# Modulation vectors of a hybrid block: column sums on VectorE in place of chunk products on TensorE, low parts of the input stage on GpSimd

## The chip, the cores and the metric

One core of a Trainium2 chip runs the whole program. The metric is device time in microseconds, taken over runs of the kernel; a profiled execution gives the trace that the rows below come from.

## The reference, cut to what matters

Two layers, each a token mixer (state-space scan, pooling, attention) and a router with experts (PEER). What the change touches is the modulation: six vectors per layer of 1024 features, each a product of one conditioning vector with a matrix.

```python
cond = jax.nn.silu(c)                       # (1, 1024)
for l in range(DEPTH):                      # 2 layers
    mod = cond @ ada_w[l] + ada_b[l]        # 1024 x 6144
    sh1, sc1, g1, sh2, sc2, g2 = jnp.split(mod, 6, axis=-1)
    h = modulate(rms_norm(x, mix_norm_g[l]), sh1, sc1)      # h * (1 + sc) + sh
    mix = token_mixer(h, w_in[l], ...)                      # begins with h @ w_in
    x = x + g1[:, None, :] * mix
    h = modulate(rms_norm(x, ffn_norm_g[l]), sh2, sc2)
    x = x + g2[:, None, :] * peer_ffn(h, peer_wq[l], ...)
return rms_norm(x, final_norm_g)
```

There are 512 tokens of 1024 features. Features lie on the 128 partitions, in KT = 8 tiles.

## The kernel before

**Weights.** All products with weights are streamed in tiles of 128x1024 (`wst`, the loop of `load_w` on SyncE, three buffers `w_raw`). Each tile is split in two: ScalarE rounds it to a high part (`hi`, `w_hi`), and another engine subtracts to get the low part (`lo`, `w_lo`); both have two buffers, so the parts of tile n wait until TensorE has done tile n-2. A projection (`project`) is 24 products: high by high, high by low, low by high. The input stage is 18 such tiles per layer: 6 for the convolved channels, 2 for pooling, 4 for the gate z, 6 for attention. Tiles 0 and 1 are done together (`project_pair`), because they follow the normalised input `hH`, `hL` feature tile by feature tile. VectorE makes all low parts, except those of 37 tiles per layer in the gate stage that follows the router; there GpSimd makes them.

**What VectorE does in the input stage.** After tile n it runs step n: convolution (`conv`, n < 6), time steps (n = 4, 5: `time_step_exp`, `time_step_log`), scaled x (n = 6, 7: `x_scaled`), decay segments and scan matrices (`segments`, `scan_matrix`, n from 8 on), pooled means (n = 9 to 11) and attention scores. In each step it also makes the low part of tile n+2. TensorE takes the results between two tiles: `decay_sums` and `x_tokens` after tile 6, `scan_step` after tiles 9, 11, 13, 15, `pool_mixed` after tile 12.

**Modulation.** The six vectors are three sets of two. One set is 8 chunks of 128x2048 (1 MB). A chunk is multiplied on TensorE with one column of silu(c) repeated over 32 columns (`ada_chunk`), four matmuls into four column groups of a bank, summed over the chunks. ScalarE then copies the bank (`ada_rows`) and TensorE transposes it (`modulation`), since the sums lie along the free axis and are wanted along the partitions. Set 0 of layer 0 (shift and scale of the first normalisation) is needed before anything else: its chunks are loaded first, half of them from SyncE's queue and half from GpSimd's, and multiplied around the sums of squares. Sets 1 and 2 of layer 0 are 16 chunks, one after the first pair and one after nearly every projection of layer 0's input stage. All 24 chunks of layer 1 are done in layer 0: five in the gap before the router (the normalisation of the second half), nineteen between router tiles. Layer 1 has no chunks, and finds its vectors in `mod_raw`.

**Order.** Every engine's program is written out by hand and runs in order; semaphores join them. `unread` are matmuls whose results nobody reads, which fill TensorE's waits. On TensorE `s_tile` counts tiles done, on the others `s_wh` and `s_wl` the high and low parts.

## Time and profile before

| | us |
|---|---|
| median of three runs | 2833.79 |
| lowest of the runs | 2832.2 |
| the profiled execution | 2832.66 |
| its span on the core | 2830.8 |
| first products of the first pair begin | 38.75 |
| input stage of layer 0, from the end of the pair | 139.9 |
| the same of layer 1 | 123.9 |

The span runs from the first to the last instruction of the core; the profiled execution's own time has 1.9 us around it. Stages are read from the timeline of TensorE, whose order is fixed by the program: the first record of a kind in a stage gives its start.

### The profile page before, as it was taken

To read this page: it belongs to the slowest core of one execution; us is meant where nothing else is said; L and a number is where in the kernel's file an instruction comes from. 1 tells how busy PE (TensorE), PEld (TensorE's weight loads), DVE (VectorE), ACT (ScalarE), POOL (GpSimd) and SP (SyncE) were. 2 spreads that over 40 slices of the span, in tenths; PEclk is the share of its full clock that TensorE was granted. 3 is DMA by queue.
4 is the path that set the end of the run, shared out by engine and by line. 5 is a ranking of instruction groups with operands and counts; after the bars stand their busy time and mean duration, and the time that the engine had idled before them with its cause. 6 is when DMAs were issued, how large, how long until landed. Compare 5 with 4: busy or idle time off the path is not lost.

```text
span 2830.8 us, 49106 instructions
## 1 busy us (share of the span) xinstructions
PE 2788.0 (98%) x17864; PEld 2594.5 (92%) x17864; DVE 2494.8 (88%) x5020; ACT 1388.2 (49%) x2321; POOL 952.1 (34%) x773
## 2 busy tenths in 40 slices
PE   7999999999999999999999999999999999999998
PEld 4777789999999999999988788999999999999998
DVE  4667789999999799999987679999999979999998
ACT  3345225477777433333353532445777753333333
POOL 1000018833335244444400000694333434444342
PEclk9999999999999999999999999999999999999999
DMA  7434648999999899999932122699999999999996
GB/s 276 181 119 179 246 157 305 353 334 403 395 380 350 333 383 385 391 391 393 392 122 74 60 74 83 219 349 332 386 386 391 364 337 368 388 390 380 385 385 260
DMA packets 257144, 855.06 MB, mean 302 GB/s; under 512 B 26080, under 2 KB 59104, under 8 KB 250336
## 3 DMA queue, kind: packets, MB, share of 16 engines
q1 hardware_dynamic: 149280, 442.23, 42.3%
q0 software_dynamic: 98496, 381.73, 35.6%
q10 hardware_dynamic: 9216, 29.36, 2.6%
q8 instruction: 61, 1.00, 0.1%
q14 instruction: 91, 0.75, 0.1%
HBM read 777.06 MB, written 76.15 MB: 301 GB/s over the span
## 4 chain that ended last, share of the span: by engine, by line
PE 74%; DVE 12%; DMA 5%; issue 4%; POOL 2%; ACT 2%; SPq 0%; DVEq 0%; ACTq 0%; POOLq 0%
PE banks L1099 36%; PE banks L1633 9%; PE banks L1636 9%; PE banks L1640 9%; DMA w_raw<-wst 4%; PE banks L1597 3%; PE banks L1434 2%; DVE stages L2193 2%; DVE w_lo L1693 2%; DVE vacc L2205 1%; POOL w_lo L756 1%; PE banks L1171 1%; PE banks L1117 1%; POOL stages L769 1%; PE banks L1521 1%
## 5 line engine op out<-in xcount | busy, mean ns | idle before, releaser
L811 ACT ACTIVATE w_hi<-w_raw 128x1024 fp32r<-128x1024 f32 x596 | 628.4, 1055 | 635.7 <-PE banks L1099 322.8
L1693 DVE TENSOR_TENSOR w_lo<-w_raw,w_hi 128x1024 fp32r<-128x1024 f32 x522 | 638.0, 1222 | 236.4 <-ACT w_hi L811 189.8
L769 POOL DMA_INDIRECT ring<-v,gidx x320 | 393.5, 1230 | 612.9 <-DVE vacc L2205 523.5
L1099 PE MATMUL banks<-hH,w_hi 128*128 128x352 f32 (+1 forms) x2528 | 513.9, 345 | 0.6 <-ACT act_out L1025 0.5
L1099 PE MATMUL banks<-hH,w_lo 128*128 128x352 f32 (+1 forms) x2528 | 492.1, 336 | 2.2 <-DVE w_lo L1693 1.5
L1099 PE MATMUL banks<-hL,w_hi 128*128 128x352 f32 (+1 forms) x2528 | 491.4, 336 | 0.0
L1099 PEld LDWEIGHTS banks<-hH,w_hi 128*128 128x128 f32 x2528 | 416.2, 188 | 37.8 <-issue 10.8
L1099 PEld LDWEIGHTS banks<-hH,w_lo 128*128 128x128 f32 x2528 | 427.7, 188 | 22.9 <-DVE w_lo L1693 2.1
L1099 PEld LDWEIGHTS banks<-hL,w_hi 128*128 128x128 f32 x2528 | 428.1, 188 | 19.0
L769 POOL DMA_INDIRECT ring<-u,gidx x244 | 282.4, 1157 | 453.4 <-DVE gact L2193 442.5
L2205 DVE SCALAR_TENSOR_TENSOR vacc<-ring,gcoef,vacc 128x1024 f32<-128x1024 f32 x316 | 404.4, 1280 | 7.1
L756 POOL TENSOR_TENSOR w_lo<-w_raw,w_hi 128x1024 fp32r<-128x1024 f32 x74 | 178.2, 2408 | 407.5 <-PE banks L1099 406.5
L1636 PE MATMUL banks<-c_lo_late,w_hi 128*128 128x352 f32 x1520 | 273.3, 322 | 0.0
L1636 PEld LDWEIGHTS banks<-c_lo_late,w_hi 128*128 128x128 f32 x1520 | 247.6, 188 | 0.0
L1017 ACT ACTIVATE oneh<-oneh,gate_pow 128x128 bf16<-128x128 f16 x704 | 221.4, 392 | 4.2 <-ACT stages L1053 3.2
L1073 ACT ACTIVATE c_hi_late<-coef 128x352 fp32r<-128x352 f32 x128 | 63.9, 499 | 316.6 <-DVE coef L2402 316.6
L2193 DVE CUSTOM_DVE_ANT_0 ring<-ring,banks 128x1024 f32<-128x1024 f32 x180 | 214.4, 1212 | 0.1
L1633 PE MATMUL banks<-c_hi_first,w_hi 128*128 128x352 f32 x1024 | 183.8, 322 | 0.0
L1640 PE MATMUL banks<-c_hi_first,w_lo 128*128 128x352 f32 x1024 | 183.8, 322 | 0.0
L1633 PE MATMUL banks<-c_hi_late,w_hi 128*128 128x352 f32 x1008 | 181.4, 322 | 1.0 <-ACT w_hi L811 1.0
L1640 PE MATMUL banks<-c_hi_late,w_lo 128*128 128x352 f32 x1008 | 180.9, 322 | 0.0
L1073 ACT ACTIVATE c_hi_first<-coef 128x352 fp32r<-128x352 f32 x124 | 61.9, 499 | 240.6 <-DVE coef L2402 240.6
(360 smaller groups left out, 3923.0 us busy)
## 6 DMA issues: line engine op xcount, KB each, us to landing
w_raw<-wst SPq DMA_DIRECT2D x596, 512.0 KB, 6.6
activations<-act_out SPq DMA_DIRECT2D x124, 352.0 KB, 8.4
act_in<-activations SPq DMA_DIRECT2D x62, 704.0 KB, 7.3
gate_matrices<-stages ACTq DMA_DIRECT2D x64, 448.0 KB, 7.6
gates<-gate_matrices SPq DMA_DIRECT2D x64, 448.0 KB, 9.4
ada_buf<-adaw POOLq DMA_DIRECT2D x24, 1024.0 KB, 6.8
nrm<-adaw POOLq DMA_DIRECT2D x8, 1024.0 KB, 5.2
pj<-adaw POOLq DMA_DIRECT2D x7, 1024.0 KB, 7.1
```

The source lines that it names most:

```text
L756: pool.tensor_tensor(w_lo[g % 2][:, :, :].rearrange("p a b -> p (a b)"), w_raw[:, g % RAWS, :], w_hi[g % 2][:, :, :].rearrange("p a b -> p ...
L769: pool.indirect_dma_start(out=gather_slot(l, k), out_offset=None, in_=rows[:, :], in_offset=bass.IndirectOffsetOnAxis(ap=gidx[:, k % UG:k ...
L811: nc.scalar.activation(w_hi[g % 2][:, :, :].rearrange("p a b -> p (a b)"), w_raw[:, g % RAWS, :], ACT.Copy).then_inc(s_wh, 1)
L1017: ins = nc.scalar.activation(oh.bitcast(BF16), oh, ACT.Copy, scale=gate_pow[:, at:at + 1])
L1073: nc.scalar.activation(c_hi[(b + 2) % GROUP], coef[:, b % 2, :], ACT.Copy).then_inc(s_chi, 1)
L1099: last = mm(bank[s][:, 0:t.stop - t.start], a[s][:, k, :], b[:, k, t], start=(k == 0 and a is w_hi and b is hH), stop=(k == KT - 1 and a i ...
L1633: mm(bank[k][:, TG:T], w_hi[j % 2][:, k, :], c_hi[j], start=first, stop=False)
L1636: last = mm(bank[k][:, TG:T], w_hi[j % 2][:, k, :], c_lo[j], start=False, stop=False)
L1640: last = mm(bank[k][:, TG:T], w_lo[j % 2][:, k, :], c_hi[j], start=False, stop=False)
L1693: v.tensor_tensor(w_lo[g % 2][:, :, :].rearrange("p a b -> p (a b)"), w_raw[:, g % RAWS, :], w_hi[g % 2][:, :, :].rearrange("p a b -> p (a ...
L2193: v.tensor_tensor_reduce(row, row, rhs, 1.0, 0.0, ALU.mult, ALU.add, gact[:, k:k + 1]).then_inc(s_gd, 1)
L2205: ins = v.scalar_tensor_tensor(acc[:, :], row, gcoef[:, k:k + 1], acc[:, :], ALU.mult, ALU.add)
```

## The change

Three things are altered.

Set 0 of layer 0 comes in another order of its matrix: chunk k now holds, for all 1024 rows, the 128 shifts and 128 scales of feature tile k. `first_block(k)` multiplies it (32 matmuls of 64 columns), VectorE takes its values out of the bank by a masked sum (`first_scaled`) and scales feature tile k, and `first_pair` follows tile by tile. All eight chunks are loaded from SyncE's queue, after the first two weight tiles' place in it.

Sets 1 and 2 of both layers are no longer chunks on TensorE. Their matrix is stored transposed, feature on the partition, and silu(c) is spread over all partitions (`crow`). A `column_sum` on VectorE multiplies a row of 128x1024 with `crow` and sums it along the free axis, straight into a column of `mod_raw`. There are 32 per layer, in steps 2 to 15 of that layer's own input stage (`ROWS_AT`), and each row is loaded by SyncE between weight tiles (`ROW_LOAD`) into parts of `nrm`, `h32` and `pj`. Of layer 1's set 0 the eight chunks stay on TensorE in layer 0: five in the gap, three in the router.

The low parts of tiles 2 to 18 of each layer move from VectorE to GpSimd.

```diff
-ADA_CHUNKS = ADA_SETS * KT
+ADA_CHUNKS = KT
 ADA_BANK = ((7, 7, 7), (5, 6, 7))
-FIRST_ADA = (0, 2, 1, 4, 3, 6, 5, 7)
-assert sorted(FIRST_ADA) == list(range(KT))
+ADA_BLOCK = ADA_COLS // KT
+ADA_FOUR = ADA_BLOCK // 4
+FIRST_BANK = (7, 6, 4)
...
+LATER = 2 * ADA_COLS // P
+ROWS_AT = {2: 2, 3: 2, 4: 1, 5: 1, 6: 3, 7: 3, 8: 2, 9: 3, 10: 2, 11: 4, 12: 2, 13: 3, 14: 2, 15: 2}
...
+ROW_LOAD = {3: (0, 1), 4: (2, 3), 5: (4, 5), 6: (6, 7, 8), 7: (9, 10), 8: (11, 12), 9: (13, 14, 15), 10: (16, 17),
...
+        def row_home(j):
+            i = ROW_PLACE[j]
+            if i < 2:
+                return nrm[:, 2 * i:2 * i + 2, :].rearrange("p a t -> p (a t)")
+            if i < 4:
+                return h32[:, 2 * i - 4:2 * i - 2, :].rearrange("p a t -> p (a t)")
+            if i < 6:
+                return pj[:, Q0:Q0 + 4, :].rearrange("p a t -> p (a t)")[:, (i - 4) * D:(i - 3) * D]
+            return h32[:, 6:8, :].rearrange("p a t -> p (a t)") if i == 6 else h32[:, 4:6, :].rearrange("p a t -> p (a t)")
...
+            def load_rows(l, n):
+                if n == 3:
+                    if l > 0:
+                        sp.wait_ge(s_x, l * KT)
+                    else:
+                        sp.wait_ge(s_adat, KT)
+                    sp.wait_ge(s_rows, 2 * l + 1)
+                    sp.dma_start(crow[:, :], cB).then_inc(s_cin, 16)
+                if n == 5:
+                    sp.wait_ge(s_dtg, l + 1)
+                for j in ROW_LOAD[n]:
+                    if j >= 8:
+                        sp.wait_ge(s_mdot, l * LATER + row_before(j) + 1)
+                    sp.dma_start(row_home(j), adaw[l, KT + j // 2][:, j % 2 * D:(j % 2 + 1) * D]).then_inc(row_in(l, j)[0], 16)
...
-            for k in (1, 3, 5, 7):
+            for k in range(KT):
                 sp.dma_start(ada_place(k), adaw[0, k]).then_inc(s_ada0[k], 16)
-            load_w(0, 0)
-            load_w(0, 1)
+                if k == 0:
+                    load_w(0, 0)
+                    load_w(0, 1)
...
+                    if n in ROW_LOAD:
+                        load_rows(l, n)
...
-            for k in (0, 2, 4, 6):
-                pool.dma_start(ada_place(k), adaw[0, k]).then_inc(s_ada0[k], 16)
...
+                for n in range(2, OUT0 + 1):
+                    if n == 2:
+                        pool.wait_ge(s_wl, l * STREAM + 2)
+                    lo(l, n)
...
+                    if n == Q0:
+                        act.wait_ge(s_mdot, l * LATER + 12)
...
+                    if n == 1:
+                        act.wait_ge(s_cin, (l + 2) * 16)
+                        nc.scalar.activation(crow[:, :], crow[:, :], ACT.Silu).then_inc(s_cond, 1)
...
+                def first_block(k):
+                    pe.wait_ge(s_ada0[k], 16)
+                    for c in range(KT):
+                        for g in range(4):
+                            o = c * ADA_BLOCK + g * ADA_FOUR
+                            last = mm(bank[FIRST_BANK[k % 3]][32 * g:32 * g + 32, k * ADA_FOUR:(k + 1) * ADA_FOUR],
+                                      tiny[:, 0, c:c + 1].broadcast_to([P, 32]),
+                                      ada_place(k)[:, o:o + ADA_FOUR], start=(c == 0), stop=(c == KT - 1))
+                    last.then_inc(s_adat, 1)
+                def first_pair(k):
+                    if k == 0:
+                        pe.wait_ge(s_wh, 2)
+                        pe.wait_ge(s_wl, 2)
+                        pe.wait_ge(s_taken, 2)
+                    pe.wait_ge(s_rhs, k + 1)
+                    for s in range(2):
+                        for a, b in ((w_hi, hH), (w_hi, hL), (w_lo, hH)):
+                            last = mm(bank[s][:, :], a[s][:, k, :], b[:, k, :],
+                                      start=(k == 0 and a is w_hi and b is hH),
+                                      stop=(k == KT - 1 and a is w_lo))
+                        if k == KT - 1:
+                            last.then_inc(s_tile, 1)
...
                 if l == 0:
-                    for c in FIRST_ADA[0:3]:
-                        ada_chunk(0, c)
                     pe.wait_ge(s_const, 11)
-                norm_groups(2 * l)
-                if l == 0:
-                    ada_chunk(0, FIRST_ADA[3])
-                if l == 0:
-                    for c in FIRST_ADA[4:7]:
-                        ada_chunk(0, c)
-                if l > 0:
+                    unread(10)
+                    norm_groups(0)
+                    unread(4)
+                    first_block(0)
+                    norm_rows(0)
+                    unread(6)
+                    first_block(1)
+                    for k in range(KT):
+                        if k + 2 < KT:
+                            first_block(k + 2)
+                        first_pair(k)
+                else:
+                    norm_groups(2 * l)
                     unread(8)
-                norm_rows(2 * l)
-                if l == 0:
-                    unread(5)
-                    ada_chunk(0, FIRST_ADA[7])
-                    unread(3)
-                    modulation(0, 0, 4)
-                    unread(13)
-                else:
+                    norm_rows(2 * l)
                     unread(10)
-
-                project_pair(l, 0, l * RHS_PARTS)
-                if l == 0:
-                    ada_chunk(0, KT)
+                    project_pair(l, 0, l * RHS_PARTS)
...
-                    if l == 0 and n != KT + 1:
-                        ada_chunk(0, KT + n - 1 if n <= KT else KT + n - 2)
...
-                    pe.wait_ge(s_arow, ADA_SETS)
-                    modulation(0, 1, 7)
-                    modulation(0, 2, 7)
...
-                        for c in chunks_of(n):
-                            ada_chunk(1, c)
+                        if GAP_ADA + n < KT:
+                            ada_chunk(GAP_ADA + n)
                         if n == 7:
-                            modulation(1, 0, 4)
+                            modulation()
...
-                    modulation(1, 1, 4)
-                    modulation(1, 2, 4)
...
+            def first_modulated():
+                ada_b, g_mix = pcol("ada_b"), pcol("g_mix")
+                def first_scaled(k):
+                    dve.wait_ge(s_adat, k + 1)
+                    for m in range(2):
+                        o = k * ADA_FOUR + m * EXTRA
+                        ins = v.tensor_tensor_reduce(tiny[:, 9 + m, :], bank[FIRST_BANK[k % 3]][:, o:o + EXTRA], token_of[:, :], 1.0, 0.0,
+                                                     ALU.mult, ALU.add, tiny[:, 8, 2 * k + m:2 * k + m + 1])
+                    link(ins)
+                    v.tensor_scalar(mod[:, 0, k:k + 1], tiny[:, 8, 2 * k:2 * k + 1], ada_b[:, k:k + 1], None, ALU.add)
+                    link(v.scalar_tensor_tensor(gs[:, 0, k:k + 1], tiny[:, 8, 2 * k + 1:2 * k + 2],
+                                                ada_b[:, KT + k:KT + k + 1], g_mix[:, k:k + 1], ALU.add, ALU.mult))
+                    v.scalar_tensor_tensor(h32[:, k, :], x[:, k, :], gs[:, 0, k:k + 1], bank[2][:, :],
+                                           ALU.mult, ALU.mult).then_inc(s_nrm, 1)
+                dve.wait_ge(s_const, 16)
+                dve.wait_ge(s_rows, 1)
+                first_scaled(0)
+                lo(0, 1)
+                for k in range(KT):
+                    if k + 1 < KT:
+                        first_scaled(k + 1)
+                    dve.wait_ge(s_hh, k + 1)
+                    v.scalar_tensor_tensor(hL[:, k, :], h32[:, k, :], mod[:, 0, k:k + 1],
+                                           hH[:, k, :].bitcast(F32), ALU.add, ALU.subtract).then_inc(s_rhs, 1)
...
+                def column_sum(j):
+                    if j == 0:
+                        dve.wait_ge(s_cond, l + 2)
+                    dve.wait_ge(*row_in(l, j))
+                    row = row_home(j)
+                    v.tensor_tensor_reduce(row, row, crow[:, :], 1.0, 0.0, ALU.mult, ALU.add,
+                                           mod_raw[:, 2 * KT + j:2 * KT + j + 1]).then_inc(s_mdot, 1)
...
-                        lo(l, n + 2)
...
+                    for _ in range(ROWS_AT.get(n, 0)):
+                        column_sum(summed)
+                        summed += 1
...
+                dve.wait_ge(s_mdot, (l + 1) * LATER)
```

VectorE in layer 0's input stage, steps 2 to 4, before (L1693 is the low part; L1786 to L1791 a convolution; L1799 to L1803 the time steps):

```order
L1693 TENSOR_TENSOR w_lo<-w_raw,w_hi 128x1024
L1786 TENSOR_SCALAR xbc<-pj,par 128x512
L1789 SCALAR_TENSOR_TENSOR xbc<-pj,par,xbc 128x512 x2
L1791 SCALAR_TENSOR_TENSOR xbc<-pj,par,xbc 128x512
L1693 TENSOR_TENSOR w_lo<-w_raw,w_hi 128x1024
L1786 TENSOR_SCALAR xbc<-pj,par 128x512
L1789 SCALAR_TENSOR_TENSOR xbc<-pj,par,xbc 128x512 x2
L1791 SCALAR_TENSOR_TENSOR xbc<-pj,par,xbc 128x512
L1799 TENSOR_TENSOR tiny<-banks,par 128x32
```

The same place after (L1984 is a column sum and the read of its accumulator):

```order
L1835 TENSOR_SCALAR xbc<-pj,par 128x512
L1838 SCALAR_TENSOR_TENSOR xbc<-pj,par,xbc 128x512 x2
L1840 SCALAR_TENSOR_TENSOR xbc<-pj,par,xbc 128x512
L1984 ISA nrm,mod_raw<-nrm,crow 128x1024
L1984 ISA mod_raw 128x1
L1984 ISA nrm,mod_raw<-nrm,crow 128x1024
L1984 ISA mod_raw 128x1
L1835 TENSOR_SCALAR xbc<-pj,par 128x512
L1838 SCALAR_TENSOR_TENSOR xbc<-pj,par,xbc 128x512 x2
L1840 SCALAR_TENSOR_TENSOR xbc<-pj,par,xbc 128x512
L1984 ISA pj,mod_raw<-pj,crow 128x1024
L1984 ISA mod_raw 128x1
```

The low part of each step is gone from VectorE, and one to four column sums stand behind each step's own work.

GpSimd's queue after the constants, before: chunk loads up to the gate stage.

```order
L732 AFFINE_SELECT tri_lt<-tri_lt 128x128
L746 DMA nrm<-adaw 128x2048
L746 DMA pj<-adaw 128x2048
L746 DMA nrm<-adaw 128x2048
L746 DMA pj<-adaw 128x2048
```

And after: the input stage's low parts, then the loads of layer 1's eight chunks, then the gate stage's low parts.

```order
L764 AFFINE_SELECT tri_lt<-tri_lt 128x128
L778 TENSOR_TENSOR w_lo<-w_raw,w_hi 128x1024 x17
L771 DMA ada_buf<-adaw 128x2048 x3
L771 DMA pj<-adaw 128x2048 x2
L771 DMA ada_buf<-adaw 128x2048 x3
L778 TENSOR_TENSOR w_lo<-w_raw,w_hi 128x1024 x9
```

Seventeen low parts stand where loads stood, and 16 of the 24 loads for layer 1 are gone.

## Rows read from the trace of the kernel before

**Rows 1.** The page: busy time, share of span, instructions, by engine
```profile
PE 2788.0 (98%) x17864; PEld 2594.5 (92%) x17864; DVE 2494.8 (88%) x5020; ACT 1388.2 (49%) x2321; POOL 952.1 (34%) x773
```

**Rows 2.** Windows, input stages: length, PE, PEld, DVE, ACT, POOL busy; clock, DMA
```profile
51.40:191.30 139.90, 139.90 (x765) 99.87 (x764) 84.47 (x142) 54.30 (x69) 7.39 (x14) 1.00 0.47 174
1461.40:1585.30 123.90, 122.16 (x638) 98.29 (x638) 84.22 (x143) 52.02 (x67) 0.00 (x0) 1.00 0.21 73
```

**Rows 3.** Chain, then timeline (start, length): last chunk, first pair; square sums
```profile
4.51 26.39 DMA pj<-adaw
...
38.75 12.80 PE banks L1117 x48
...
21.44 2.72 PE L1131 MATMUL banks<-h,ones 128*32 128x128 f32 x64
```

**Rows 4.** Window at the start, ending in GB/s; landing of keys, of w_raw
```profile
8.00:10.00 2.00, 0.00 (x0) 0.00 (x0) 0.66 (x6) 0.72 (x2) 0.00 (x0) 1.00 1.02 434
...
DMA to landing us min/median/max: 4.8/4.8/4.8
...
DMA to landing us min/median/max: 3.1/6.6/27.9
```

**Rows 5.** Timeline of TensorE, layer 0: the first output block begins
```profile
207.55 0.47 PE L1434 MATMUL banks<-hH,w_hi 128*128 128x512 f32 x1 [0.66 <-DVE hL L2054]
```

**Rows 6.** Timeline of TensorE, layer 1: attention sums, first output block
```profile
1588.66 3.57 PE L1404 MATMUL banks<-nlk,neg_ge 128*128 128x512 f32 x8 [2.37 <-DVE nlk L2010]
...
1602.74 0.47 PE L1434 MATMUL banks<-hH,w_hi 128*128 128x512 f32 x1 [0.20 <-issue]
```

**Rows 7.** Timeline of TensorE, routers, layer 0 then 1: scores, transpositions
```profile
285.57 1.05 PE L1521 MATMUL banks<-keys,qT 128*128 128x128 f32 x8
...
319.40 1.06 PE L1521 MATMUL banks<-keys,qT 128*128 128x128 f32 x8
...
326.97 1.06 PE L1521 MATMUL banks<-keys,qT 128*128 128x128 f32 x8
...
408.23 1.07 PE L1572 MATMUL banks<-ident,h 128*128 128x128 f32 x8
...
1680.55 1.06 PE L1521 MATMUL banks<-keys,qT 128*128 128x128 f32 x8
...
1686.92 1.06 PE L1521 MATMUL banks<-keys,qT 128*128 128x128 f32 x8
...
1779.08 1.04 PE L1572 MATMUL banks<-ident,h 128*128 128x128 f32 x8
```

**Rows 8.** Gather sums; VectorE's low parts (window); GpSimd's (ns min/median/max)
```profile
465.30 1.22 DVE L2193 CUSTOM_DVE_ANT_0 stages<-stages,banks 128x1024 f32<-128x1024 f32 x1
...
466.44 1.22 DVE L2193 CUSTOM_DVE_ANT_0 stages<-stages,banks 128x1024 f32<-128x1024 f32 x1
...
1461.40:1585.30 123.90, 20.80 (x17) 1.00 0.21 73
...
L756 POOL TENSOR_TENSOR w_lo<-w_raw,w_hi x74: 2352/2409/2437, 402.1 to 1922.2; 128x1024 fp32r<-128x1024 f32 x74
```

**Rows 9.** Timeline, gate stage: GpSimd's low part beside VectorE; the gates' product
```profile
448.97 2.40 POOL L756 TENSOR_TENSOR w_lo<-w_raw,w_hi 128x1024 fp32r<-128x1024 f32 x1
...
450.08 0.29 DVE L2301 TENSOR_TENSOR posu<-narrow,banks 128x128 uint32<-128x128 f32 x1
450.40 1.13 DVE L2302 TENSOR_TENSOR posu<-bestp,posu 128x128 uint32<-128x128 uint32 x1
...
L2333 DVE TENSOR_TENSOR route<-bestv,gsum x6: 292/1012/2580, 468.1 to 1923.8; 128x128 f32<-128x128 f32 x6
```

**Rows 10.** Windows of layer 1's input stage; last, VectorE's low parts alone
```profile
1461.40:1492.60 31.20, 31.20 (x154) 24.63 (x154) 24.95 (x43) 16.73 (x23) 0.00 (x0) 1.00 0.26 89
...
1502.00:1543.60 41.60, 41.03 (x229) 33.73 (x227) 29.36 (x49) 11.95 (x18) 0.00 (x0) 1.00 0.18 63
...
1461.40:1492.60 31.20, 7.33 (x6) 1.00 0.26 89
```

More of the change, by code:

```diff
@@ L189 @@
 PAIR_K = 5
-def chunks_of(n):
-    return [GAP_ADA + 2 * n, GAP_ADA + 2 * n + 1] if n < 4 else [n + 9]
-assert [c for n in range(N_Q - 1) for c in chunks_of(n)] == list(range(GAP_ADA, ADA_CHUNKS))
+LATER = 2 * ADA_COLS // P
+ROWS_AT = {2: 2, 3: 2, 4: 1, 5: 1, 6: 3, 7: 3, 8: 2, 9: 3, 10: 2, 11: 4, 12: 2, 13: 3, 14: 2, 15: 2}
+assert sum(ROWS_AT.values()) == LATER
+ROW_PLACE = (0, 1, 4, 5, 2, 3, 6, 7, 0, 1, 4, 5, 2, 3, 6, 7, 0, 1, 2, 3, 6, 7, 0, 1, 2, 3, 6, 0, 1, 2, 3, 6)
+ROW_LOAD = {3: (0, 1), 4: (2, 3), 5: (4, 5), 6: (6, 7, 8), 7: (9, 10), 8: (11, 12), 9: (13, 14, 15), 10: (16, 17),
+            11: (18, 19), 12: (20, 21, 22), 13: (23, 24), 14: (25, 26, 27), 15: (28, 29), 16: (30, 31)}
+assert [j for n in sorted(ROW_LOAD) for j in ROW_LOAD[n]] == list(range(LATER)) and len(ROW_PLACE) == LATER
 Y_BANK = (3, 4, 5, 2)
@@ L291, in ada_place, with row_before, row_in @@
                 return first_ada[:, n - 3, :]
-            if n < KT:
-                rows = Z0 if n == 6 else Q0
-                return pj[:, rows:rows + 4, :].rearrange("p a t -> p (a t)")[:, 0:ADA_COLS]
-            if n % 2 == 0:
-                return nrm[:, :, :].rearrange("p a t -> p (a t)")
-            if n < 2 * KT:
-                return pj[:, Q0:Q0 + 4, :].rearrange("p a t -> p (a t)")[:, 0:ADA_COLS]
-            return h32[:, 0:4, :].rearrange("p a t -> p (a t)")
+            rows = Z0 if n == 6 else Q0
+            return pj[:, rows:rows + 4, :].rearrange("p a t -> p (a t)")[:, 0:ADA_COLS]
+        def row_home(j):
[7 more added lines that the diff above has]
+            return h32[:, 6:8, :].rearrange("p a t -> p (a t)") if i == 6 else h32[:, 4:6, :].rearrange("p a t -> p (a t)")
+        def row_before(j):
+            return max(i for i in range(j) if ROW_PLACE[i] == ROW_PLACE[j])
+        def row_in(l, j):
+            i = ROW_PLACE[j]
+            return s_ada0[i], 16 * (1 + l * ROW_PLACE.count(i) + ROW_PLACE[:j + 1].count(i))
         def pcol(name, n=None):
@@ L462, in build @@
         sb("to_rows", [P, 29728 - 29056], where=late)
-        ada_row = [sb(f"ada_row{s}", [P, T], where=late) for s in range(2)]
+        ada_row = sb("ada_row", [P, T], where=late)
         late.close()
-        def row_place(n):
-            return h32[:, 5 + n, :] if n in (1, 2) else ada_row[n % 2][:, :]
+        over_row = ExitStack()
+        sb("row_pad", [P, 29728], where=over_row)
+        crow = sb("crow", [P, D], where=over_row)
+        over_row.close()
         before_att = ExitStack()
@@ L1170, in ada_chunk @@
                     for j in range(ADA_GROUPS):
-                        last = mm(bank[ADA_BANK[at][i]][32 * j:32 * j + 32, :],
-                                  tiny[:, 0, k:k + 1].broadcast_to([P, 32]),
-                                  ada_place(n)[:, j * T:(j + 1) * T], start=(k == first), stop=(k == final))
+                        last = mm(bank[5][32 * j:32 * j + 32, :], tiny[:, 0, c:c + 1].broadcast_to([P, 32]),
+                                  ada_place(n)[:, j * T:(j + 1) * T], start=(c == 0), stop=(c == KT - 1))
@@ L1716, in modulated @@
                 scaled(1)
-                if l == 0 and which == 0:
-                    lo(0, 1)
                 for k in range(KT):
@@ L1965, in _ @@
                         zs_from(1, ((6, 0),), (0,)).then_inc(s_zv, 1)
-                    else:
-                        lo(l, n + 2)
                     if n < CONVS:
```

98 lines of the change are left out of this document (34 added, 64 removed).

## The prediction

> **What bounds the kernel now.** I read the page first: TensorE is busy for 2788.0 us of the 2830.8, 98% [rows 1]. So the question for every edit is whether it takes work off TensorE, and whether TensorE then waits for something else. The next view is the one by stages. The input stage (from the end of the first pair of tiles to the end of tile 17) takes 139.9 us in layer 0 and 123.9 us in layer 1 [rows 2]. The 16.0 us between them are the 16 modulation chunks that only layer 0 has: 1.0 us each. TensorE has no gap there, VectorE works 84 us in both, GpSimd does nothing. That makes layer 1 of this trace a measured picture of layer 0 without its chunks. The same comparison serves in the router. Last I looked at what VectorE and GpSimd do to each other where both work at once, because the change makes them do so in a new place.
>
> **The start.** Before, the last of eight 1 MB chunks lands at 30.9, then come its multiplication, a row copy, a transposition, the gains and the first products; the 48 records of the first pair run from 38.75 for 12.80 us, to 51.5 [rows 3]. After, a feature block needs one chunk only, and pair steps run between blocks. A block is 32 matmuls of 64 columns into four column groups; nearest are the square sums, 32 matmuls of 128 columns, 64 records in 2.72 us early in the program [rows 3]. I take 2.0; 1.0 is the lower end, since the columns are half and TensorE has been at work for longer by then. A pair step is six tile products at 0.23 us of spacing, 1.4 us. Arrival: the queues together move 434 GB/s [rows 4]; at that, the 5.5 MB that precede and include block 1 are in at 15 to 16. Square sums, block 0 and the root rows keep TensorE until about 18.5. From there to the end of block 7 stand 7 blocks and 5 pair steps, 14 + 7 = 21 us, so about 40. Block 7 is then followed by two short reductions, two column operations, the scaled product (0.74), the high part (0.72) and the low part (0.74), with hand-overs 3.5 us, which hides steps 5 and 6, and step 7 (1.4): 45. Tile 0 now ends only 0.7 us before tile 1, so the next high part is late by 0.5. The end of the pair moves from 51.5 to 45.5: **-6**. Bounds: all loads are now on one queue. There 1 MB landed in 4.8 us and half a MB in 3.1 at best [rows 4], which leaves 3.4 us per MB, the last chunk at about 40 and the pair's end at 47 to 48; with blocks of 1.0 us it is 42. So -3 to -10.
>
> **Layer 0, sixteen chunks and two transpositions off TensorE.** From the first product after the pair to the first output block: before 51.55 [rows 3] to 207.55 [rows 5], 156.0 us. Layer 1, without chunks and transpositions: 1461.4 [rows 2] to 1602.74, 141.3 us, with the wait of 2.37 us for VectorE's attention work that then shows [rows 6]. So **-14.7**, if VectorE keeps up as well as it does in layer 1 now.
>
> **Router of layer 0.** From the first scores to the transpositions before the gate stage: 285.57 to 408.23, 122.7 us; in layer 1 1680.55 to 1779.08, 98.5 us [rows 7]. A step with one chunk has a spacing of 7.57 us, one without 6.37: 1.2 us per chunk there. After the change three chunks and one of three transpositions (0.9) stay: 98.5 + 3.6 + 0.9 = 103.0. **-19.6**. VectorE's top-k work is the same in both layers, and layer 1 shows that it allows the spacing of 6.37. The chunks in the gap before the router stay and cost nothing new.
>
> **What VectorE gets, in both layers.** Thirty-two column sums of 128x1024: the gathers' sums have the same form, and two in a row start 1.14 us apart [rows 8]. 36.5 us. What it loses: 17 low parts, 20.8 us. Its work in layer 1's stage goes from 84.2 to 84.2 - 20.8 + 36.5 = 99.9 us in 123.9 [rows 2, 8]. By itself that fits. The rows to be summed are loaded by SyncE between weight loads, and SyncE waits for earlier sums; by my count of the steps a weight load is then issued up to 9 us later than now and still lands 7 us before its high part, so this costs nothing unless sums run late by more than that.
>
> **What GpSimd gets.** A low part takes it 2.41 us [rows 8]. It can start 1.2 us after tile n-2 ends and is wanted 9 us after that end, so its own lateness is covered by 5 us. But look at VectorE next to such a low part. At 448.97 GpSimd starts one and ends it at 451.37. VectorE's operations with one operand in PSUM go on at 0.29 us; the one at 450.40, both of whose inputs are in SBUF, takes 1.13 us and ends 0.16 us after GpSimd does. The product of the gates, again with two SBUF inputs, ranges from 292 ns to 2580 ns [rows 9]. So VectorE is shut out of such an operation for the rest of GpSimd's low part. In the gate stage it hardly matters, because nearly all of VectorE's operands there are in PSUM. In the input stage convolutions, scan matrices, pooling and the new column sums all read two SBUF tensors; I estimate these at three quarters of its 100 us.
>
> The price, per layer: 17 x 2.4 = 41 us of port time. A part meets VectorE idle or on a PSUM operand. If each low part costs it 1.9 us, VectorE needs 99.9 + 32 = 132 us in a stage of 123.9: +8. Hand-overs and TensorE's slow restart after waits come on top: after the wait of 2.37 us in layer 1 the next products took 3.57 us [rows 6]. +5. I take **+13 for each layer, +26**. The lower bound is 0 (VectorE's operations keep ahead, GpSimd's parts fall into its gaps); the upper is worked out below.
>
> The Trainium skill has this as a rule that speaks against the change: "SBUF — State Buffer", section "Who interferes with whom", says that a VectorE instruction with two SBUF inputs and a GpSimd instruction that reads SBUF exclude each other for the whole instruction, whichever came first. Rows 9 agree for VectorE's side. Nothing in this trace shows GpSimd arriving while VectorE has many such operations in a row; by the page GpSimd would wait for one of them at most, and the sum would go to its upper end.
>
> **Sum.** -6 - 14.7 - 19.6 + 26 = -14.3. The profiled execution took 2832.66 us, 1.1 below the median of 2833.8; on the median that is **2819 us**. Two per cent of this kernel, about what a measurement of it can tell from no change, is 57 us, far more than any case here.
>
> **Rivals.**
> (a) *VectorE keeps up*: the low parts fall into its waits, or its operations, each following the last at once, leave GpSimd no opening until it is idle. For it: 24 us idle in each stage, and 5 us of cover for GpSimd. Against: in rows 9 it was VectorE that waited. -6 - 14.7 - 19.6 = -40.3, and -1 for a wait for the scaled x that goes: 2792.
> (b) *The port chain makes it slower than before*: every low part costs VectorE its 2.4 us, and the loss falls where TensorE waits for a chain. Place: the sums of time steps wanted after tile 6. In the first 31.2 us of the stage VectorE works 24.95, of it 7.33 on low parts [rows 10]. 24.95 - 7.33 + 5 sums x 1.14 + 7 x 2.4 = 40.1: 9 us late. Then the segments wanted before the pooled product at tile 12: in the 41.6 us up to them VectorE works 29.36 [rows 10]; less five low parts (6.1), plus 12 column sums (13.7) and 5 x 2.4 = 12 of shut-out that is 49: 7 us late, and it starts behind. With the tail of the stage and restarts I get +21 to +23 per layer: -40.3 + 44 = +4, 2837. It decides from 20.2 us per layer upward (40.3 / 2).
> (c) *The start gives nothing*: one queue is slower, or blocks at the early rate of 2.72 us hold TensorE. 0 to +3 in place of -6: 2825 to 2828 on the forecast.
> (d) *It doesn't take the work away*: excluded, the instruction order shows the chunks gone from TensorE.
>
> **How the numbers follow.** Forecast with +8 to +18 per layer, 2808 to 2830: 0.48. (a) with its start bounds, 2786 to 2800: 0.25. (b) 2831 to 2843: 0.19. (c) 0.05, others 0.03. The range 2789 to 2841 leaves out the ends of (a) and (b). All cases lie within 2%: faster by more 0.01, within 0.98, slower by more 0.01.
>
> **What the changed profile would show.** Right: stage of layer 1 longer than 123.9 by 8 to 18 us, TensorE waiting in it for VectorE's time steps and segments; convolution and column-sum operations whose maximum is 2 to 3 us while their minimum is 0.75 and 1.2; router steps at 6.37; the pair's end near 45. Wrong: column sums all at 1.2 us and a stage of 124 mean (a); waits at tile 6 of 9 us in both layers mean (b); a last chunk landing after 38 is (c). The prediction fails altogether if SyncE's waits delay weight loads, which would show as ScalarE waiting for w_raw in the input stage.

## The result, and the profile after

The changed kernel takes 2836.23 us (median; 2832.64 to 2841.34) against 2830.75 us before (12 runs of each): ratio 1.002, 95% interval 1.0012 to 1.0028. It is slower by 0.2%, where 14 us less were forecast. One of the twelve runs before took 4590 us; the other eleven lie between 2828.5 and 2833.8 us, and without it the median is the same within 0.1 us. The profiled execution took 2835.72 us, its span 2833.9 us.

The page of the changed kernel, first part: busy time, share of the span and instructions.

```profile
PE 2763.2 (98%) x18014; PEld 2597.8 (92%) x18014; DVE 2588.5 (91%) x5161; ACT 1386.2 (49%) x2318; POOL 1020.5 (36%) x771
```

TensorE is busy 24.8 us less than in [rows 1] and the span is 3.1 us longer: what came off TensorE turned into waits. VectorE has 93.7 us more. The stages say where. Their bounds are starts in TensorE's timeline, in microseconds; "stage" is from the first products of tile 2 to the first output block.

| | before | after | difference |
|---|---|---|---|
| start to tile 2, layer 0 | 52.5 | 43.8 | -8.7 |
| stage, layer 0 | 155.1 | 164.6 | +9.5 |
| router, layer 0 (scores to transpositions) | 122.7 | 103.1 | -19.6 |
| stage, layer 1 | 141.3 | 164.5 | +23.2 |
| router, layer 1 | 98.5 | 98.5 | 0 |

The sum is +4.4; the profiled executions differ by 3.1 us and the medians by 5.5, the rest is spread over the long stages. In the kernel before, one chunk product (1.0 us) stands between the end of the pair and tile 2 of layer 0, so its removal counts in the first row here; the forecast counted it among the sixteen chunks.

TensorE's waits in layer 1's stage, before and after the change (view of waits; us in total, times, longest):

```profile
PE banks L1404 <- DVE nlk L2010: 2.4, 1, 2.4
PE banks L1243 <- DVE xdt L1840: 1.2, 1, 1.2
PE banks L1324 <- DVE seg L1867: 0.6, 1, 0.6
```

```profile
PE banks L1357 <- DVE seg L1916: 7.4, 1, 7.4
PE banks L1276 <- DVE xdt L1889: 5.7, 1, 5.7
PE banks L1276 <- ACT xbc L892: 4.8, 1, 4.8
PE banks L1435 <- DVE nlk L2070: 2.7, 1, 2.7
```

Before, the last of these was the large one [rows 6]. The other three are now 17.9 us, where 1.8 us stood before: for the convolved channels and the scaled x around tile 6 (`x_tokens`, after tiles 5 and 6), and for the segments ahead of `pool_mixed` at tile 12. All lead back to VectorE; the activation of L892 itself had waited for a convolution. All of TensorE's waits in the stage are 21.0 us after and 4.2 before, 16.8 more. The rest of the 23.2 is in TensorE's own time: the same 733 records are busy for 143.3 us instead of 137.0, 6.3 more, at a lower granted clock. The windows of layer 1's stage, columns as in [rows 2], the granted clock behind POOL's busy time:

```profile
1484.00:1494.00 10.00, 4.94 (x21) 4.54 (x22) 9.93 (x17) 3.06 (x7) 2.37 (x1) 0.66 0.46 150
...
1534.00:1544.00 10.00, 3.76 (x17) 2.79 (x15) 9.82 (x19) 0.00 (x0) 0.00 (x0) 0.80 0.85 283
1544.00:1554.00 10.00, 8.81 (x24) 5.83 (x25) 9.96 (x14) 5.88 (x6) 3.42 (x1) 0.69 0.34 102
...
1444.10:1608.60 164.50, 143.27 (x733) 113.13 (x733) 143.00 (x209) 64.64 (x80) 43.60 (x17) 0.92 0.45 150
```

VectorE has hardly an idle moment where TensorE waits. TensorE's granted clock is a mean of 0.66 to 0.80 in those stretches, between its levels of 2.4 and 1.2 GHz, and 0.92 over the stage, where it was 0.99 before. After the wait of 7.4 us the four records of the pooled product take 3.75 us, before they took 1.96.

VectorE's timeline beside GpSimd's low parts at the stage's begin, changed kernel, layer 1 (start, length):

```profile
1448.73 0.54 DVE L1835 TENSOR_SCALAR xbc<-pj,par 128x512 f32<-128x512 f32 x1
...
1453.38 2.53 POOL L778 TENSOR_TENSOR w_lo<-w_raw,w_hi 128x1024 fp32r<-128x1024 f32 x1 [4.86 <-ACT w_hi L837]
...
1453.69 2.77 DVE L1840 SCALAR_TENSOR_TENSOR xbc<-pj,par,xbc 128x512 f32<-128x512 f32 x1
...
1459.20 3.42 DVE L1984 CUSTOM_DVE_ANT_0 nrm<-nrm,crow 128x1024 f32<-128x1024 f32 x1
...
1472.21 2.34 POOL L778 TENSOR_TENSOR w_lo<-w_raw,w_hi 128x1024 fp32r<-128x1024 f32 x1 [10.67 <-ACT w_hi L837]
...
1472.59 2.25 DVE L1835 TENSOR_SCALAR xbc<-pj,par 128x512 f32<-128x512 f32 x1 [2.79 <-ACT pj L925]
```

The convolution's last operation takes 2.77 us where it needs 0.75, the column sum 3.42 where it needs 1.22. The operation of L1835 reads only one tensor of 128x512 from SBUF (and a column of `par`), and it too is held up: beside GpSimd's part, which ends at 1474.55, it takes 2.25 us, and ends at 1474.84, where it needs 0.54.

### The profile page after: what moved, and what is told of

It is laid out like the page before. It is cut to its first block, busy times and chain, and to the rows that moved or that the text cites. A ratio compares the mean times of both kernels' runs of the same rounds, so it can differ in the third digit from the quotient of the medians.

```text
span 2833.9 us, 49610 instructions
## 1 busy us (share of the span) xinstructions
PE 2763.2 (98%) x18014; PEld 2597.8 (92%) x18014; DVE 2588.5 (91%) x5161; ACT 1386.2 (49%) x2318; POOL 1020.5 (36%) x771
## 4 chain that ended last, share of the span: by engine, by line
PE 67%; DVE 24%; issue 4%; DMA 3%; ACT 2%; SPq 0%; DVEq 0%; ACTq 0%
PE banks L1120 31%; PE banks L1657 9%; PE banks L1654 9%; PE banks L1661 8%; DVE stages L2250 3%; PE banks L1618 3%; DMA w_raw<-wst 2%; DVE vacc L2262 2%; PE banks L1465 2%; DVE w_lo L1714 1%; DVE h L1984 1%; DVE pick L2370 1%; DVE pick L2374 1%; PE banks L1546 1%; DVE xbc L1838 1%
## 5 line engine op out<-in xcount | busy, mean ns | idle before, releaser
L1714 DVE TENSOR_TENSOR w_lo<-w_raw,w_hi 128x1024 fp32r<-128x1024 f32 x488 | 596.4, 1222 | 124.3 <-ACT w_hi L837 91.4
L778 POOL TENSOR_TENSOR w_lo<-w_raw,w_hi 128x1024 fp32r<-128x1024 f32 x108 | 267.5, 2478 | 604.4 <-PE banks L1120 329.4
```

What stands on the lines that cost most here:

```text
L778: pool.tensor_tensor(w_lo[g % 2][:, :, :].rearrange("p a b -> p (a b)"), w_raw[:, g % RAWS, :], w_hi[g % 2][:, :, :].rearrange("p a b -> p ...
L1714: v.tensor_tensor(w_lo[g % 2][:, :, :].rearrange("p a b -> p (a b)"), w_raw[:, g % RAWS, :], w_hi[g % 2][:, :, :].rearrange("p a b -> p (a ...
```

## The experiments

Ten kernels were run. The stage (tile 2 to first output block, layer 0 / layer 1) is read from TensorE's timeline as above. In layer 1 before, and in both layers of `neither` below, it is 141.3 to 141.6 us; this is the stage without either cost, and the losses below are counted from it. Each ratio is to the runs of the kernel before that were taken along with that run (medians 2829.7 to 2831.6).

| run | low parts of the stage on | column sums | time | ratio to before (interval) | stage, layers 0 / 1 |
|---|---|---|---|---|---|
| changed kernel | GpSimd | full | 2836.23 | 1.002 (1.0012 to 1.0028) | 164.6 / 164.5 |
| `lo_dve` | VectorE | full | 2824.23 | 0.9972 (0.9962 to 0.9981) | 157.1 / 158.2 |
| `lo_late` | VectorE, from tile 13 GpSimd | full | 2826.69 | 0.9986 (0.9976 to 0.9995) | 159.2 / 159.0 |
| `no_sums` | GpSimd | one column | 2804.30 | 0.9901 (0.9885 to 0.9918) | 147.7 / 147.9 |
| `before_pool` | GpSimd in layer 1 | none (kernel before) | 2837.64 | 1.0022 (1.0013 to 1.0032) | 155.1 / 148.0 |
| `neither` | VectorE | one column | 2791.46 | 0.9861 (0.9845 to 0.9878) | 141.6 / 141.6 |
| `half_sums` | VectorE | 512 columns | 2807.82 | 0.9925 (0.9908 to 0.9942) | 151.3 / 149.9 |
| `spread` | VectorE | full, later steps | 2869.45 | 1.0138 (1.0121 to 1.0155) | 180.5 / 180.6 |
| `ends` | VectorE | full, end of step | 2825.75 | 0.9979 (0.997 to 0.9989) | 156.2 / 159.0 |
| `gaps` | VectorE | full, ahead of the low part | 2810.59 | 0.9925 (0.9911 to 0.9938) | 149.6 / 151.9 |
| `two_queues` | GpSimd | full | 2844.80 | 1.0058 (1.0041 to 1.0075) | 163.7 / 162.9 |

**`lo_dve`: the low parts back on VectorE.** `POOL_IN` is the tuple of tiles whose low part GpSimd makes, here empty.

```diff
-                for n in range(2, OUT0 + 1):
-                    if n == 2:
-                        pool.wait_ge(s_wl, l * STREAM + 2)
+                for n in POOL_IN:
+                    pool.wait_ge(s_wl, l * STREAM + n)
                     lo(l, n)
...
+                    elif n + 2 not in POOL_IN:
+                        dve.wait_ge(s_wl, l * STREAM + n + 2)
+                        lo(l, n + 2)
                     if n < CONVS:
```

> The changed kernel with the low parts of tiles 2 to 18 back on VectorE; sums, loads and start stay. Theory P (the port chain: each low part on GpSimd holds up VectorE's next operation for about 2 us, and TensorE waits for VectorE's chains at tiles 6 and 12): without GpSimd's parts VectorE needs 84.2 + 36.8 = 121 us in a stage of 124, 30.7 of 31.2 us up to the time steps and 43 of 41.6 us up to the pooled product. The waits of 4.8, 5.7 and 7.4 us nearly go, 2 to 5 us per layer are left; start (-8.7) and chunks (-14.7, -19.6) show: 2792 to 2800. Rival S (the sums alone: 36.8 us of new work standing ahead of what TensorE waits for, whoever makes the low parts; VectorE with the low parts has 20.8 us more of its own): the waits stay at 15 us or more per layer, 2828 to 2838.

Neither theory as it stood. The stage shortens by 7.5 and 6.3 us, and 15 to 17 us above 141.3 stay. GpSimd's low parts are a third of the loss at most; the sums make the rest. In this kernel a wait of 8.2 us stands at tile 12.

**`lo_late`: only tiles 13 to 18 on GpSimd** (`POOL_IN = tuple(range(13, 19))`).

> The changed kernel with the low parts of tiles 2 to 12 on VectorE and those of tiles 13 to 18 on GpSimd. P: the early chains are as without GpSimd's parts; six low parts fall where VectorE has idle time, so each frees 1.2 us and costs up to 2: within 3 us of the run with all low parts on VectorE, 2790 to 2803. S: 2826 to 2838, like the changed kernel.

It lies 2.5 us from `lo_dve`, with stages 1 to 2 us longer: giving low parts to GpSimd brings nothing even where VectorE has more room. The level expected was wrong with that of `lo_dve`.

**`no_sums`: the sums cut, GpSimd's low parts kept.**

```diff
-                    v.tensor_tensor_reduce(row, row, crow[:, :], 1.0, 0.0, ALU.mult, ALU.add,
-                                           mod_raw[:, 2 * KT + j:2 * KT + j + 1]).then_inc(s_mdot, 1)
+                    v.tensor_tensor(mod_raw[:, 2 * KT + j:2 * KT + j + 1], row[:, 0:1], crow[:, 0:1],
+                                    ALU.mult).then_inc(s_mdot, 1)
```

> The changed kernel with each column sum cut to one product of 128x1, so sets 1 and 2 hold wrong values; row loads and GpSimd's low parts stay. P: VectorE's own work is 63.4 us and 17 shut-outs of 2 us make 97 of 124 us; up to the time steps 17.6 + 14 = 31.6 of 31.2 us. So 0 to 4 us per layer, 2787 to 2796, with single VectorE operations still at 2 to 3 us. S: no wait at all, 2786 to 2790, and no such long operations would be needed. A third theory L (the row loads on SyncE's queue delay the weights): the waits stay although the sums are gone, above 2805.

The stage is 6.4 to 6.6 us above 141.3, more than the 0 to 4 expected, and the wait of 4.8 us for the scaled x at tile 6 (1.2 before) is that of GpSimd's parts alone. The time is above the 2787 to 2796 expected. The wait at tile 12 is gone. ScalarE has no wait for w_raw; L was to be told by that, and by a time above 2805 (it is 2804.3).

**`before_pool`: GpSimd's low parts alone, in layer 1 of the kernel before.**

```diff
+                else:
+                    for n in range(2, OUT0 + 1):
+                        if n == 2:
+                            pool.wait_ge(s_wl, l * STREAM + 2)
+                        lo(l, n)
...
-                    else:
+                    elif l == 0:
                         lo(l, n + 2)
```

> The kernel before with the low parts of tiles 2 to 18 of layer 1 on GpSimd, nothing else. P: each costs VectorE about 2 us where it meets an operation on SBUF; VectorE's busy time in layer 1's input stage goes from 84.2 less 20.8 = 63.4 to between 80 and 97 us, still inside 124, and the time stays within 0 to +4 us of the kernel before. If GpSimd's parts cost VectorE nothing it is 63 to 66 us. S says nothing of the busy time, and no change of the time.

Slower by 7 us, where 0 to 4 were expected: 148.0 us in place of 141.3, and layer 0 as before. VectorE's busy time, kernel before and this one, each from the stage's begin to the first output block (the last one ends 0.8 us short of it):

```profile
1461.40:1602.70 141.30, 136.97 (x733) 109.22 (x732) 98.13 (x162) 63.72 (x79) 0.00 (x0) 0.99 0.21 70
```

```profile
1461.70:1609.00 147.30, 139.17 (x730) 110.89 (x730) 97.41 (x144) 63.93 (x79) 40.88 (x17) 0.97 0.20 66
```

Seventeen low parts of 1.22 us (20.8) went from VectorE, and its busy time hardly fell. 97.41 - (98.13 - 20.8) = 20.1 us, and 20.8 with the missing 0.8 us of the stage: each of GpSimd's parts cost VectorE 1.2 us, as much as making it. The time is also in a worse place: VectorE's timeline of this run, with one of GpSimd's early low parts among its rows,

```profile
1460.85 5.58 DVE L1781 TENSOR_SCALAR h<-h,mod 128x512 f32<-128x512 f32 x3
...
1471.31 2.77 DVE L1796 SCALAR_TENSOR_TENSOR xbc<-pj,par,xbc 128x512 f32<-128x512 f32 x1
...
1476.32 2.84 POOL L756 TENSOR_TENSOR w_lo<-w_raw,w_hi 128x1024 fp32r<-128x1024 f32 x1 [2.79 <-ACT w_hi L816]
...
1476.82 2.63 DVE L1791 TENSOR_SCALAR xbc<-pj,par 128x512 f32<-128x512 f32 x1
...
1487.85 3.75 DVE L1794 SCALAR_TENSOR_TENSOR xbc<-pj,par,xbc 128x512 f32<-128x512 f32 x2
```

shows it in the last operations of the normalised input (`h`) and in the convolutions. Behind these VectorE makes the scaled x, for which TensorE then waits 4.7 us (1.2 before).

**`neither`: low parts on VectorE, sums cut.** The two edits above together.

> The changed kernel with low parts on VectorE and each column sum cut to one product of 128x1 (sets 1 and 2 hold wrong values); start, chunks off TensorE and row loads stay. If the two costs found so far (6.6 us per layer for GpSimd's low parts, 16.9 for the sums) are all there is, TensorE needs 141.3 us from tile 2 to the first output block as layer 1 did before, and the time is 2830.6 - 8.7 - 14.7 - 19.6 = 2788 (2785 to 2792). If the row loads on SyncE's queue or on the DMA engines cost something, the stage is longer than 142 us and ScalarE waits for w_raw: 2793 or more.

The stage is 141.6 us in both layers. So the chunks' removal and the row loads do what was forecast, the rows' DMAs cost TensorE 0.3 us at most, and the two costs are the loss in layer 1: 141.6 + 6.3 (`no_sums`) + 16.6 (`lo_dve`) = 164.5, measured 164.5. In layer 0 they give 141.6 + 6.1 + 15.5 = 163.2, and 164.6 was measured; 1.4 us come only when both are there. The time of 2791.5 is 3.5 us above the 2788 expected; 1.0 of that is the chunk between the pair and tile 2, which the expectation took off twice, in the 8.7 and in the 14.7.

**`half_sums`: sums over 512 columns.**

```diff
-                    v.tensor_tensor_reduce(row, row, crow[:, :], 1.0, 0.0, ALU.mult, ALU.add,
+                    v.tensor_tensor_reduce(row[:, 0:T], row[:, 0:T], crow[:, 0:T], 1.0, 0.0, ALU.mult, ALU.add,
```

> As the run lo_dve, with each column sum over 512 of 1024 features (0.6 us in place of 1.15; sets 1 and 2 hold wrong values). Theory D (VectorE's work summed up to a place where TensorE waits is too much there, though not in the stage as a whole): up to the pooled product 29.4 + 12 x 0.6 = 36.6 of 41.6 us, so the wait of 8.2 us at tile 12 goes nearly altogether, the waits around tile 6 halve, and a layer loses 2 to 6 us instead of 16.9: 2792 to 2801. Theory O (order alone: each sum stands ahead of something TensorE waits for and delays it by its own length, whatever the total): half of 16.9 is left, 8 to 9 us per layer, 2804 to 2807.

8.6 us stay in layer 1 (10 in layer 0), O's number of 8 to 9; D's 2 to 6 is missed, and the wait at tile 12 is 4.2 us where D had it nearly gone. The loss goes in step with the sums' length: in layer 1 VectorE's busy time is 34.1 us above that of `neither` in `lo_dve` and 17.1 above it here, and the stage is 16.6 and 8.3 us longer. O's wording, that each sum delays TensorE by its own length, is not borne out: the delay is half of it. But sums of half the length are not free either, even where VectorE has work for 36.6 of 41.6 us. How that can be is seen in VectorE's timeline of layer 1 in the kernel before, the low parts of tiles 9 to 13 with the idle time ahead of each, then TensorE's pooled product:

```profile
1502.72 1.22 DVE L1693 TENSOR_TENSOR w_lo<-w_raw,w_hi 128x1024 fp32r<-128x1024 f32 x1 [4.54 <-ACT w_hi L811]
...
1511.81 1.23 DVE L1693 TENSOR_TENSOR w_lo<-w_raw,w_hi 128x1024 fp32r<-128x1024 f32 x1 [3.94 <-ACT w_hi L811]
...
1517.25 1.23 DVE L1693 TENSOR_TENSOR w_lo<-w_raw,w_hi 128x1024 fp32r<-128x1024 f32 x1 [3.01 <-ACT w_hi L811]
...
1527.03 1.23 DVE L1693 TENSOR_TENSOR w_lo<-w_raw,w_hi 128x1024 fp32r<-128x1024 f32 x1 [1.76 <-ACT w_hi L811]
...
1532.50 1.22 DVE L1693 TENSOR_TENSOR w_lo<-w_raw,w_hi 128x1024 fp32r<-128x1024 f32 x1 [1.28 <-ACT w_hi L811]
...
1542.20 1.96 PE L1324 MATMUL banks<-pooled,par 128*128 128x512 f32 x4 [0.57 <-DVE seg L1867]
```

VectorE's idle time lies ahead of the low parts, where it waits for a high part that waits for TensorE. Behind the low part of tile 13 it works without a stop up to the segments, and TensorE already waited 0.57 us for them: no room there. The change put four sums exactly there, at the end of step 11, and seven more in steps 8 to 10. VectorE and TensorE in `lo_dve`:

```profile
1523.68 1.22 DVE L1984 CUSTOM_DVE_ANT_0 h<-h,crow 128x1024 f32<-128x1024 f32 x1
...
1524.82 1.22 DVE L1984 CUSTOM_DVE_ANT_0 h<-h,crow 128x1024 f32<-128x1024 f32 x1
...
1525.97 1.22 DVE L1984 CUSTOM_DVE_ANT_0 h<-h,crow 128x1024 f32<-128x1024 f32 x1
...
1527.11 1.22 DVE L1984 CUSTOM_DVE_ANT_0 nrm<-nrm,crow 128x1024 f32<-128x1024 f32 x1
...
1533.21 0.43 DVE L1916 TENSOR_SCALAR seg<-seg 128x512 f32<-128x512 f32 x1
...
1533.78 3.75 PE L1357 MATMUL banks<-pooled,par 128*128 128x512 f32 x4 [8.20 <-DVE seg L1916]
```

**`spread`: seven sums moved behind tile 12.** `lo_dve` with

```diff
-ROWS_AT = {2: 2, 3: 2, 4: 1, 5: 1, 6: 3, 7: 3, 8: 2, 9: 3, 10: 2, 11: 4, 12: 2, 13: 3, 14: 2, 15: 2}
+ROWS_AT = {2: 1, 3: 1, 4: 1, 5: 1, 6: 1, 7: 2, 8: 3, 9: 2, 10: 2, 11: 2, 12: 3, 13: 4, 14: 4, 15: 5}
```

and the row loads and places that go with it.

> As the run lo_dve, with the 32 sums of a layer at other steps: 4 up to step 5 (were 6), 3 in steps 6 and 7 (were 6), 9 in 8 to 11 (were 11), 16 in 12 to 15 (were 9); same work. D: the lateness at tile 12 shrinks by the 7 sums that are now behind it, 8 us; those at tile 6 by 2 to 5 sums; some of it comes back in steps 12 to 15, where VectorE had 17 us idle and now gets 8 more. A layer loses 5 to 10 us instead of 16.9: 2800 to 2811. If it is the amount of work and not its place, the time stays at 2822 to 2826.

40 us slower than the kernel before, where 20 to 30 us of gain were expected, for a reason that neither theory had: the edit's row loads. ScalarE's timeline,

```profile
1544.48 1.06 ACT L837 ACTIVATE w_hi<-w_raw 128x1024 fp32r<-128x1024 f32 x1 [11.02 <-DMA w_raw<-wst]
...
1571.59 1.06 ACT L837 ACTIVATE w_hi<-w_raw 128x1024 fp32r<-128x1024 f32 x1 [8.74 <-DMA w_raw<-wst]
```

shows it waiting for weights, 37.3 us in four waits in layer 1. With five places for rows and four sums in a step, SyncE waits for a sum that comes late before it may overwrite its row, from tile 12 on mostly one of two steps back, and the next weight tile is queued behind that wait. In the changed kernel a row load waits for no sum later than three steps back, and ScalarE never waits for w_raw in layer 1's stage. The run says nothing on D.

**`gaps` and `ends`: the same sums at two places of a step.** Both are `lo_dve` with 1, 1, 2, 2, 4, 4, 3, 3, 2, 2, 3, 2, 3 sums in steps 3 to 15 and row loads that keep the three steps; `gaps` also has

```diff
+                    for _ in range(ROWS_AT.get(n, 0)):
+                        column_sum(summed)
+                        summed += 1
                     if n < N_IN - 1:
                         dve.wait_ge(s_wl, l * STREAM + n + 2)
                         lo(l, n + 2)
...
-                    for _ in range(ROWS_AT.get(n, 0)):
-                        column_sum(summed)
-                        summed += 1
```

> As the run lo_dve, with each step's column sums ahead of its low part, where VectorE waits for the high part (2.2 to 4.5 us in steps 4, 5, 7, 8, 9 and 13 to 15 of layer 1 before), and as many per step as about fit: 1, 1, 2, 2, 4, 4, 3, 3, 2, 2, 3, 2, 3 in steps 3 to 15. Row loads wait for no later sums than in the changed kernel. Theory G (VectorE's idle time lies ahead of the low parts, a sum behind it pushes what TensorE waits for, since TensorE already waited 0.57 us for the segments at tile 12): what exceeds the gaps is 7 us up to tile 12, so a layer loses 4 to 9 us instead of 16.9: 2798 to 2808. If only the amount of work counts: 2822 to 2826.

> The same numbers of sums per step as the run gaps, but at the end of each step as in the changed kernel. G: three sums fewer stand in steps 10 and 11, four more in 7 and 8, where 4.5 and 3.9 us are idle one step further on: a layer loses 10 to 15 us, 2810 to 2821. If the position inside the step doesn't matter, it equals the run gaps within 3 us.

`ends` equals `lo_dve` within 1.5 us, though its sums are distributed otherwise (5 us above the range expected). With fewer sums right ahead of the segments the wait at tile 12 is 3.9 us instead of 8.2 in layer 1, but the wait for the scaled x is 4.9 instead of 3.7 and one of 2.7 for a scan matrix has come (0.6 in `lo_dve`): the loss moved to other waits. So the four sums of step 11 are not by themselves what costs the time. `gaps` is 15 us faster than `ends` with the same work; the two differ only in the place of the sums inside a step. Its stages lose 8.3 and 10.6 us instead of 15.0 and 17.7: G's mechanism, a little less than its size (2810.6 us, where 2798 to 2808 were expected). In layer 1 VectorE now has no gap ahead of its low parts from step 6 to step 11. It is 0.75% faster than the kernel before (0.9925, 0.9911 to 0.9938) and faster than the changed kernel, the best version here that computes all of the reference.

**`two_queues`: the odd feature blocks on GpSimd's queue**, in the changed kernel, with semaphores of their own.

```diff
+            for k in range(1, KT, 2):
+                pool.dma_start(ada_place(k), adaw[0, k]).then_inc(s_adap[k // 2], 16)
             pool.memset(ones[:, :], 1.0).then_inc(s_const, 1)
```

> The changed kernel with the odd feature blocks of the first set loaded from GpSimd's queue instead of SyncE's. If one queue holds the start up, blocks 1 and 2 come earlier and the waits of 2.2 and 1.4 us before them go: the pair ends 2 to 3.5 us earlier, 2833 to 2834.5. If the DMA engines are full anyway, the waits stay within 0.5 us of what they were, and so does the time.

Slower than the changed kernel by 9 us (medians 2844.8 and 2836.2), where 2 to 3.5 us of gain or nothing were expected; tile 2 begins at 52.96 instead of 43.78. The windows of the start, changed kernel and this one:

```profile
20.00:25.00 5.00, 3.99 (x70) 3.33 (x70) 3.73 (x13) 1.26 (x2) 0.00 (x0) 0.66 1.01 416
```

```profile
20.00:25.00 5.00, 3.87 (x73) 3.70 (x74) 0.00 (x0) 0.10 (x1) 0.00 (x0) 0.50 1.03 422
```

The rate is the same, 416 and 422 GB/s, at a DMA share of 1.01 and 1.03 (the column before the rate): one queue already fills the DMA engines. What changes is the order. On one queue the two weight tiles arrive behind block 0, and ScalarE waits 1.0 us for weights at the start; with two queues it waits 9.1 us, until 24.9, presumably because blocks that are wanted later now share the engines with the weights:

```profile
3.65 21.23 DMA w_raw<-wst
...
24.90 1.06 ACT w_hi L840
```

(the chain of this run). The waits for blocks grew too, from 3.6 to 5.8 us.

## Why the prediction was wrong

**The start** was forecast at -6 (-3 to -10). From the end of the pair before (51.5) to the first product of tile 2 after (43.8), the places that the forecast used, it gave -7.7. The 8.7 of the table holds one of the sixteen chunks as well. The blocks of feature tiles took 1.03 us each as spaced in the timeline (27.82 to 28.85), the lower end named, not 2.0. The bound of 3.4 us per MB on one queue did not hold, the queue carried 416 to 426 GB/s from 5 to 30 us. The pair's products ended near 42.7, not 45; tile 2 then waited 1.1 us, for which 0.5 had been put.

**Chunks and transpositions off TensorE in layer 0's stage**: -14.7 forecast. By the forecast's boundaries the stage was 156.0 us before, and in `neither` it is 141.6: -14.4 us. **The router**: -19.6 forecast, -19.6 measured (122.7 to 103.1). Both right, since layer 1 of the kernel before had been a picture of layer 0 without its chunks.

**VectorE in the stages**: +13 per layer forecast, +23.1 and +23.2 measured (layer 0 against `neither`, layer 1 against before). This is the term that failed. The forecast let the column sums by themselves cost nothing, in one sentence: "By itself that fits", said of 99.9 us of work in 123.9. A loss came only with the 32 us of shut-out by GpSimd's low parts (8 us) and with restarts (5 us). The average does fit, but the sums alone cost 15.8 and 16.9 us (`lo_dve` against 141.3), and about half of that at half their length. The sentence compared a total with a length. It didn't look where VectorE's idle time lies (ahead of each low part) nor where the change puts the sums (behind it, four of them right ahead of the segments, for which TensorE waited already). That this order matters is shown by `gaps` against `ends`: the same work put ahead of the low parts takes 15 us off. [Rows 6] had shown a wait for attention work in the same stage; the wait of 0.57 us at tile 12 stands in the same timeline and was not used.

**The shut-out by GpSimd** was right in mechanism and about twice too large in its effect on the stage: the forecast lost the whole +13 with it and nothing without it, restarts included, and 6.1 to 7.5 us were measured, by `lo_dve`, `no_sums` and `before_pool`. So +13 was too much for one cause, and the larger cause had nothing. In VectorE's busy time the estimate was nearer. A part costs 1.2 us in `before_pool`. In the changed kernel, where VectorE is nearly always at work, it is 143.0 less (134.47 - 20.8), 29.3 us for 17 parts, 1.7 us each; 1.9 was estimated. Here 134.47 is `lo_dve`'s row of the same stretch, below.

```profile
1438.00:1596.20 158.20, 140.31 (x733) 111.18 (x733) 134.47 (x225) 64.66 (x80) 0.00 (x0) 0.95 0.47 156
```

The Trainium skill ("SBUF — State Buffer", "Who interferes with whom") says one thing more than the prediction used: `tensor_scalar` can enter a mode that takes the shared ports as well, when its operands meet the conditions. The runs agree with that (0.54 to 2.25 and 2.63 us for L1835 and its like, one SBUF input), though no row says in which mode an operation ran. The prediction had already taken from there that whoever comes first holds the ports, and had no row for GpSimd's side. The runs have one: GpSimd's part at 1507.98 took 3.43 us in place of 2.34, behind a VectorE operation on SBUF that had begun 0.07 us earlier. So VectorE isn't always the loser.

```profile
1507.91 1.25 DVE L2031 TENSOR_TENSOR pool_a<-pj 128x1054 f32<-128x1054 f32 x1
...
1507.98 3.43 POOL L778 TENSOR_TENSOR w_lo<-w_raw,w_hi 128x1024 fp32r<-128x1024 f32 x1 [6.75 <-ACT w_hi L837]
```

**The rivals.** (b), slower than before at 2837, comes nearest in time: 2836.2, with waits at tiles 6 and 12 as it placed them. But it is not confirmed: it charged all of its +22 per layer to the port chain, and `no_sums` shows the chain to be 6 to 7 of them. That its number came out is luck: a chain priced too high stood in for sums priced too low. Its sums already had 5 and 12 column sums in them; counted for themselves, without GpSimd, they give 43 us of work in 41.6 up to tile 12, an excess of 1.4, where 8.2 us of wait were measured. (a), 2792, is the time without either cost: `neither` has 2791.5. (c) did not occur. The fear that row loads delay weights was unfounded in the changed kernel and real in `spread`.

**Size against the clock.** Of the 23.2 us in layer 1, 16.8 are longer waits. The rest, 6.3 us, is TensorE's own records at a mean granted clock of 0.92 instead of 0.99, as in the pooled product's 3.75 us against 1.96; the forecast had put +5 "on top" for hand-overs and restarts.

Left open: how much of `gaps`'s remaining 8 to 10 us would go if sums could stand in step 16, where VectorE still idles 5.4 us ahead of its low part. This was not tried. Nor was it shown why a sum at the end of a step costs about half its length and not all or nothing.

## What to carry to other kernels

Work that is moved to an engine with idle time must be compared with the gaps by place, not in total: find what each gap waits for, put the work directly ahead of that wait, and look for the waits of the bound engine that are already above zero, since in front of those there is no room. Here the sums at the ends of the steps cost half of their time although VectorE was idle for 43 us of the stage and all of them took 37. Moving an elementwise subtraction on SBUF from VectorE to GpSimd saved VectorE nothing here (1.22 us less, 1.2 to 1.7 us more per part). And a load that waits for a consumer must not stand in the queue of the weights, unless that consumer is several steps back.

## What the runs showed of the hardware that was not expected

- A VectorE operation with only one SBUF input (TENSOR_SCALAR, 128x512) is held up by GpSimd's part as well: 2.25 to 2.63 us instead of 0.54.
- VectorE isn't always the one that is held up: a low part of GpSimd's took 3.43 us instead of 2.34 behind a VectorE operation.
- The cost of GpSimd's parts and that of the sums add almost exactly in layer 1 (6.3 and 16.6 us alone, 22.9 together, above `neither`) and within 1.4 us in layer 0.
- One DMA queue carried 416 to 426 GB/s from 5 to 30 us, as much as two (413 to 427); with the second the first weights came later and the start was 9.2 us longer.
